# Layer 0's output projection in two PSUM banks in turn, more places for scores, and a new written order of the first fourteen positions

## What is computed

```python
out = concatenate([fourier_mix(f), ssd_out(y, z)], -1) @ w_out     # 1536 -> 1024
x = x + gate1 * out
h = rms_norm(x) * (1 + scale) + shift
# PEER, for each token and each of 8 heads
s = einsum("thsd,hskd->thsk", (h @ wq), keys)        # two sides, 128 scores each
s_top, i_top = top_k(s, 16)
g_score, c_idx = top_k(all 256 sums of one of each side, 16)
experts = e1 * 128 + e2;  gates = softmax(g_score)
act = gelu(u[experts] . h) * gates                   # 16 rows of u a head
y = sum(act * v[experts])                            # 16 rows of v a head
x = x + gate2 * y
```

## Time and profile before

| | us |
|---|---|
| median of 3 runs | 4380.73 (4378.84 to 4380.82) |
| the profiled execution | 4392.34 |
| its span | 4390.3 |
| layer 0's gathers are issued | 621.7 to 2678.8 |
| layer 1's gathers are issued | 3043.5 to 4357.3 |
| granted TensorE clock, mean | 0.843 |

### The profile page before, as it was taken

One profiled execution on the slowest core, in us unless ns is written; L12 is line 12 of the kernel. 1 busy time (PEld: TensorE's weight loads), 2 busy tenths in 40 slices (PEclk: granted clock), 3 DMA queues, 4 the chain that ended last, 5 costly groups with the idle time before them and its releaser, 6 DMA issues. The chain is left out here.

```text
span 4390.3 us, 37624 instructions
## 1 busy us (share of the span) xinstructions
PE 3099.0 (71%) x12112; PEld 1320.1 (30%) x12112; DVE 2858.1 (65%) x7086; ACT 1127.3 (26%) x2971; POOL 1579.2 (36%) x1383
## 2 busy tenths in 40 slices
PE   7999988776766765555566667999886755555555
PEld 3655543332322221111222213565432311111111
DVE  2524754789888988555555555565788898555554
ACT  1122521332322322111222212563332322111111
POOL 0002412344444455444444441001444454444443
PEclk9999998888887887777788878999987877777777
DMA  4114746799999999999999996103999999999998
GB/s 172 39 39 148 256 182 254 284 420 419 418 420 404 420 418 420 422 420 415 408 421 416 421 421 258 39 1 134 392 420 420 417 421 416 420 422 418 419 420 338
DMA packets 223656, 1471.78 MB, mean 335 GB/s; under 512 B 25436, under 2 KB 29244, under 8 KB 53220
## 3 DMA queue, kind: packets, MB, share of 16 engines
q0 software_dynamic: 184320, 1342.26, 74.0%
q1 hardware_dynamic: 37764, 123.17, 7.8%
q10 hardware_dynamic: 1376, 3.96, 0.2%
HBM read 1467.02 MB, written 2.28 MB: 335 GB/s over the span
## 5 line engine op out<-in xcount | busy, mean ns | idle before, releaser
L1911 PE MATMUL banks<-arena 128*64 128x512 f32 x5120 | 1640.6, 800 | 1188.0 <-ACT arena L2145 1132.0
L1643 POOL DMA_INDIRECT arena<-experts,arena x1280 | 1503.4, 1175 | 2293.8 <-PE banks L1911 1556.6
L2298 DVE CUSTOM_DVE_ANT_0 arena<-arena 128x1024 f32<-128x1024 f32 x1280 | 1535.0, 1222 | 834.1 <-DMA arena<-experts,arena 828.5
L1911 PEld LDWEIGHTS banks<-arena 128*64 128x64 f32 x5120 | 450.6, 182 | 2303.7 <-ACT arena L2145 1317.7
L2139 ACT ACTIVATE arena<-arena 128x4 f32<-128x4 f32 x320 | 66.1, 207 | 2296.1 <-DVE arena L2298 2279.8
L2145 ACT ACTIVATE arena<-arena 128x64 f32<-128x64 f32 x1280 | 340.4, 336 | 37.2 <-ACT arena L2139 1.2
L1734 PE MATMUL banks<-arena 128*128 128x512 f32 (+3 forms) x960 | 289.0, 456 | 6.2 <-DMA arena<-wq 5.2
L1661 PE MATMUL banks<-arena 128*128 128x512 f32 x416 | 197.2, 625 | 26.2 <-DVE arena L2191 22.4
L434 PE MATMUL banks<-arena 128*128 128x512 f32 (+1 forms) x640 | 210.1, 488 | 1.9 <-PEq L201 1.9
L871 POOL TENSOR_TENSOR arena<-arena 128x256 f32<-128x256 f32 x48 | 41.2, 859 | 433.3 <-POOLq L625 333.8
L1734 PEld LDWEIGHTS banks<-arena 128*128 128x128 f32 x960 | 160.7, 191 | 113.5 <-issue 87.9
(11 more groups left out here) (243 smaller groups left out, 2962.8 us busy)
## 6 DMA issues: line engine op xcount, KB each, us to landing
arena<-l_w_ada SPq DMA_DIRECT2D x48, 1024.0 KB, 5.0
arena<-wq SPq DMA_DIRECT2D x54, 512.0 KB
arena<-experts,arena POOLq DMA_INDIRECT x1280
arena<-l_w_in SPq DMA_DIRECT2D x7, 2048.0 KB, 7.8
arena<-l_w_out SPq DMA_DIRECT2D x4, 1536.0 KB, 8.8
arena<-l_w_o SPq DMA_DIRECT2D x4, 1024.0 KB, 9.9
arena<-keys SPq DMA_DIRECT2D x27, 128.0 KB
arena<-gates SPq DMA_DIRECT2D x6, 512.0 KB, 12.0
```

Source lines behind the costliest of these rows:

```text
L1643: pool.indirect_dma_start(slots[n], None, tbl, bass.IndirectOffsetOnAxis(ap=expert[:, ring[c], k:k + 1], axis=0)).then_inc(land[n]["sem"], ...
L1911: mm = pe.matmul(core["ps"][QS * j:QS * j + QS, c, :], diag[:, g % 2, k, :], v[:, D + c * 512:D + (c + 1) * 512], start=(g % (NB * PH) == ...
L2298: dve.tensor_tensor_reduce(u, u, rep[i // PH % 2][:, k % NQ, :], 1.0, 0.0, ALU.mult, ALU.add, dots[:, k:k + 1]).then_inc(dot["sem"], up(dot))
```

## The change

It leaves the computation and its amount as they are. In words:

- **Banks.** In layer 0, the first seven halves (up to (5,0)) go to banks 6 and 7 in turn: (0,0) 6, (0,1) 7, (1,0) 6, (2,0) 7, (3,0) 6, (4,0) 7, (5,0) 6. All the later ones, (1,1) to (5,1), are in bank 7 as before. `before_half` is now the last half before in the same bank.
- **Scores.** Events 2 to 7 of layer 0 have two tiles each and now use two of the four rows of a score buffer, by turns the upper and the lower ones; `scores_out` waits only for choices whose rows overlap. The query copy `qb` is split in two sides for events of two tiles too.
- **Order of the choices.** (4,0) comes fifth, before (2,1); seven choices instead of six, and six events instead of five, are done in the opening. The rule begins at position 14 with choice 7, so choice c is begun at position 2c where it was 2c - 1.
- **The written order** of all three engines is new. The projections stand some positions earlier on TensorE, `gate_out(5,1)` at the end of position 11 instead of 12, the dots are mingled with other work more finely, and softmaxes and diagonals on ScalarE stand in another order.

```diff
@@ PEER_MAPS, layer 0 @@
-     "order": [(0, 0), (1, 0), (2, 0), (3, 0)] + [c for h in range(4, PH) for c in ((h - 2, 1), (h, 0))] +
-              [(6, 1), (7, 1)] + [(7, t) for t in range(2, 6)] + [(0, t) for t in range(1, 6)] + [(1, 1)] +
-              [(h, t) for h in range(1, PH - 1) for t in range(2, 6)],
-     "choose_from": 11, "early": 6, "ahead": 5, ...
+     "order": [(0, 0), (1, 0), (2, 0), (3, 0), (4, 0)] + [c for h in range(5, PH) for c in ((h - 3, 1), (h, 0))] +
+              [(5, 1), (6, 1), (7, 1)] + [(7, t) for t in range(2, 6)] + [(0, t) for t in range(1, 6)] + [(1, 1)] +
+              [(h, t) for h in range(1, 5) for t in range(2, 6)] + [(5, 2), (6, 2)] +
+              [(h, t) for h in (5, 6) for t in range(3, 6)],
+     "choose_from": 14, "early": 7, "ahead": 6, "asked_from": 12, ... "halved": range(2, PH),
@@ peer_block @@
-        earlier[e] = max([n for n in range(e) if buffer_of[n] == buffer_of[e]], default=None)
+        first_tile = 2 * (e // 2 % 2) if e in m["halved"] else 0
+        rows_of[e] = range(first_tile, first_tile + len(events[e][1]))
+        before_e = [n for n in range(e) if buffer_of[n] == buffer_of[e] and set(rows_of[n]) & set(rows_of[e])]
+        earlier[e] = max([last[n] for n in before_e], default=None)
...
-    def bank_of(c):
-
+    def bank_of(t, c):
+
+        n = halves_at[t, c]
+        if layer == 0 and n <= halves_at[tiles - 1, 0]:
+            return 6 + n % 2
         return 6 + c
@@ TensorE, opening(g) @@
                 if g == 0:
+                    project(3, 0, 4, 10)
                     spread_choice(1)
-                    project(3, 0, 2, K)
-                    project(4, 0, 0, 4)
+                    project(3, 0, 10, K)
+                    project(4, 0, 0, 8)
                 if g == 1:
-                    project(4, 0, 4, K)
-                    project(5, 0, 0, 6)
+                    project(4, 0, 8, K)
+                    project(5, 0)
                 if g == 2:
-                    project(5, 0, 6, K)
                     project(1, 1)
+                    project(2, 1, 0, 4)
                 if g == 3:
-                    project(2, 1, 0, 4)
                     turn_rows(1)
-                    project(2, 1, 4, 8)
+                    project(2, 1, 4, 6)
+                    query(2, 0)
+                    project(2, 1, 6, 8)
                 if g == 4:
-                    query(2, 0)
                     query(2, 1)
-                if g == 5:
                     scores(2, 0)
                     scores(2, 1)
+                    project(2, 1, 8, 10)
                     query(3, 0)
+                    project(2, 1, 10, K)
+                    scores(3, 0)
...
@@ TensorE, the opening's rest, new @@
+                if g == 5: query(3, 1); project(3, 1, 0, 4); scores(3, 1); project(3, 1, 4, 6)
+                if g == 6: spread_choice(2); project(3, 1, 6, 10); query(4, 0); project(3, 1, 10, K)
+                if g == 7: query(4, 1); project(4, 1, 0, 4)
+                if g == 8: turn_rows(2); spread_choice(3); project(4, 1, 4, K); scores(4, 0); scores(4, 1)
+                if g == 9: project(5, 1, 0, 8)
+                if g == 10: project(5, 1, 8, K); query(5, 0)
+                if g == 11: turn_rows(3); scores(5, 0); query(5, 1); spread_choice(4)
+                if g == 12: turn_rows(4); scores(5, 1); turn_rows(5); spread_choice(5)
+                if g == 13: spread_choice(6)
@@ TensorE, ahead of position 0 @@
+                project(2, 0, 0, 2)
                 scores(1, 0)
-                project(2, 0, 0, 2)
                 scores(1, 1)
                 project(2, 0, 2, K)
-                project(3, 0, 0, 2)
+                project(3, 0, 0, 4)
@@ ScalarE, opening(g), new @@
+                if g == 0: softmax(1)
+                if g == 2: squares(1)
+                if g == 3: root(1); low_columns(1)
+                if g == 4: query_out(2, 0); query_out(2, 1); scores_out(2, 0); scores_out(2, 1); query_out(3, 0)
+                if g == 5: softmax(2); scores_out(3, 0); squares(2); query_out(3, 1)
+                if g == 6: scores_out(3, 1); root(2)
+                if g == 7: softmax(3); query_out(4, 0)
+                if g == 8: query_out(4, 1); squares(3); root(3)
+                if g == 9: scores_out(4, 0); scores_out(4, 1); squares(4); root(4)
+                if g == 10: softmax(4)
+                if g == 11: query_out(5, 0); low_columns(2); squares(5); root(5); softmax(5); query_out(5, 1)
+                if g == 12: low_columns(3); scores_out(5, 0); low_columns(4); scores_out(5, 1); softmax(6)
+                if g == 13: low_columns(5)
@@ VectorE, opening(g), new (d(a, b) stands for dot_batch(g, a, b)) @@
+                if g == 0: d(0, 4); choose_b(1); choice_out(1); gate_out(2, 0)
+                if g == 1: d(0, 1); gate_out(3, 0); d(1, 4)
+                if g == 2: d(0, 1); gate_identity(1); gate_identity(2); d(1, 2); gate_out(4, 0); d(2, 4)
+                if g == 3: d(0, 1); gate_out(5, 0); d(1, 3); gate_out(1, 1); d(3, 4)
+                if g == 4: d(0, 2); norm_rows(1); d(2, 3); high_columns(1); d(3, 4)
+                if g == 5: d(0, 1); gate_identity(3); d(1, 4); choose_a(2)
+                if g == 6: d(0, 1); gate_out(2, 1); d(1, 3); choose_b(2); d(3, 4); choose_a(3)
+                if g == 7: d(0, 1); choice_out(2); d(1, 4)
+                if g == 8: d(0, 1); norm_rows(2); gate_out(3, 1); gate_identity(4); d(1, 4); choose_b(3); gate_identity(5)
+                if g == 9: d(0, 3); norm_rows(3); high_columns(2); choice_out(3); d(3, 4)
+                if g == 10: d(0, 1); gate_out(4, 1); d(1, 2); choose_a(4); d(2, 4); norm_rows(4)
+                if g == 11: d(0, 2); choose_b(4); d(2, 4); gate_out(5, 1)
+                if g == 12: d(0, 1); choose_a(5); d(1, 3); high_columns(3); d(3, 4); gate_identity(6); choice_out(4)
+                if g == 13: d(0, 1); choose_b(5); norm_rows(5); d(1, 2); high_columns(4); choose_a(6); d(2, 3);
+                            gate_identity(7); d(3, 4); choose_b(6); choice_out(5); high_columns(5); choice_out(6)
```

More of the change, by code:

```diff
@@ L1312 @@
               [(h, t) for h in range(4) for t in range(1, 4)] + [(h, t) for t in range(2, 4) for h in range(4, PH)],
-     "choose_from": 3, "early": 2, "ahead": 4, "spread_at": (4, 5), "spread_first": (4, 5),
+     "choose_from": 3, "early": 2, "ahead": 4, "asked_from": 0, "spread_at": (4, 5), "spread_first": (4, 5),
      "halves": tuple((t, c) for t in range(TL) for c in range(2)),
-     "opening": tuple(range(8)) * 2, "ready": 8, "column": (), "near": 2,
+     "opening": tuple(range(8)) * 2, "ready": 8, "column": (), "near": 2, "halved": (),
      "w": RO + SLOT, "g1": HO + 16384, "g2": HO + 17408,
@@ L1370, in peer_block @@
     for e in range(AHEAD, E):
-        held = last[earlier[e]] if earlier[e] is not None else 0
-        query_at[e] = max(chosen_at[first[e], 0] - 5, query_at.get(e - 1, -1) + 2,
+        held = earlier[e] or 0
+        query_at[e] = max(chosen_at[first[e], 0] - 5, query_at.get(e - 1, -1) + 2, m["asked_from"],
                           chosen_at[held, 0] - 2 if held >= EARLY else 0)
@@ L1836, in opening @@
+                if g == 11:
+                    turn_rows(3)
+                    scores(5, 0)
+                    query(5, 1)
+                    spread_choice(4)
+                if g == 12:
+                    turn_rows(4)
+                    scores(5, 1)
+                    turn_rows(5)
                     spread_choice(5)
[L1837 to L1840 removed]
                 if g == 13:
[L1842 removed]
+                    spread_choice(6)
@@ L2058, in opening @@
             def opening(g):
+                if g == 0:
+                    softmax(1)
+                if g == 2:
+                    squares(1)
                 if g == 3:
-                    squares(1)
                     root(1)
@@ L2126, in _ @@
                 gate_low(3)
-                answer(1)
-                softmax(1)
+                query_out(1, 0)
+                query_out(1, 1)
+                scores_out(1, 0)
+                scores_out(1, 1)
             if layer == 1:
@@ L2404, in opening @@
+                    gate_out(3, 1)
+                    gate_identity(4)
+                    dot_batch(8, 1, 4)
                     choose_b(3)
-                    dot_batch(8, 1, 3)
-                    choice_out(3)
-                    gate_out(2, 1)
-                    dot_batch(8, 3, 4)
-                    choose_a(4)
+                    gate_identity(5)
                 if g == 9:
                     dot_batch(9, 0, 3)
-                    norm_rows(2)
-                    choose_b(4)
+                    norm_rows(3)
@@ L2436, in opening @@
-                if g == 13:
-                    dot_batch(13)
-                    norm_rows(5)
+                    choose_b(4)
+                    dot_batch(11, 2, 4)
+                    gate_out(5, 1)
+                if g == 12:
+                    dot_batch(12, 0, 1)
```

(23 more changed lines are left out.)

177 lines of the change are left out of this document (92 added, 85 removed).

## The result

The changed kernel took 4337.01 us in the median of four runs (4336.48 to 4340.26), the kernel before 4380.72 (4378.84 to 4380.82): ratio 0.9895, 95% interval 0.9883 to 0.9907. That is 43.7 us less, where 47 were forecast.

The account below looks back on a forecast made before the run. Transfers set the end, and layer 0's opening loop of slots and gathers withholds them. Gains of 16.7 + 18.3 + 16.7 less 2.1 make 49.6 us, taken as 47 off the 4380.7 median: 4334, range 4318 to 4345.

Parts of the forecast that it names:

- (a): The forecast itself: new banks and order in layer 0's opening give 4318 to 4345 us; chance 0.62.
- (b): Rival: alternated banks give nothing, since gathers end each turn anyway; the order's 32 us stay: 4349; chance 0.10.
- (d): Rival: no change, transfers not kept full after 806 us since VectorE enters position 13 late: 4381; chance 0.04.
- (e): Rival: slower, choices from position 14 wait longer for exponentials, 66 us lost against 50 gained: 4397; chance 0.04.
- (c): Rival: TensorE becomes the bound, a third of positions 4 to 9 at low clock: 24 gained, 4357; chance 0.18.
- the walk: Paper pass through each engine's written list with measured prices, over layer 0's opening: 49.6 us gained.
- to the worse side: Summed gain of 49.6 us, with 4 us better to 7 worse allowed, taken as 47.
- The clock of the forecast: Landing of the 53rd gather, first into the last five slots: the end moves with it, 49.6 us earlier.
- The banks: Positions 0 to 3: alternating banks hides the first halves, 3.7 + 13.0 = 16.7 us gained.
- Price nothing: Halved score buffers and longer `qb` only loosen waits; no VectorE or TensorE wait in the walk ends at them.
- Positions 5 to 7: TensorE's list sets these turns at 16.5, 13.3 and 13.0 us; position 5 gives back 5 us.
- The last gate: `gate_out(5,1)` closing position 11: the 53rd gather follows the 52nd by 1.3 us instead of 18.0, 16.7 gained.

Follow-up runs that it names:

- second profile: The changed kernel timed and profiled once more, nothing altered: 4340.5 us, ratio 0.9894 to the kernel before.
- four k moved: Changed kernel with four k of `project(4,1)` moved from behind block 8 to behind block 7: 4341.3 us, ratio 0.9893 to the kernel before.
- fewer k: Changed kernel with five of twelve k left out of each of halves (2,1) and (3,1): 4340.1 us, ratio 0.9888 to the kernel before.
- choice 2 early: Changed kernel with `spread_choice(2)`, `choice_out(2)` moved earlier and two k of `project(4,1)` moved behind block 7: 4343.2 us, ratio 0.9900 to the kernel before.

## Why the prediction was right, and where it was not

The time lay 3 us from the forecast, in case (a); (b), (d) and (e) did not occur. Of (c), TensorE's lists did set blocks 5, 6 and 7, as in the walk of (a), but the clock granted from 700 to 780 us was 0.96, where (c) asked for less than 0.85. A part of the closeness is luck: the walk gave 49.6, and the 2.6 us taken off it "to the worse side" had no row behind them.

**The clock of the forecast** was right, and is the best of it: the end moves with the 53rd gather. Ten kernels in eleven profiles show it. For the queue that stands before it 2.1 us were taken off; 45.9 us at the 53rd became 43.3 of length, 2.6 off (4.0 in the second profile).

**The walk.** Blocks after the first gather, forecast (with the 621.7 of before taken off) and measured: block 1 38.6 and 40.2, block 3 77.6 and 80.6, block 5 106 and 108.2, block 7 132 and 133.6, block 8 144 and 148.1, block 9 157 and 163.9, block 11 181 and 187.0, the 53rd 184.6 and 190.5. The sum of the walk, 49.6, was therefore 6 too large, and the 47 on record 3 or 4. Half of the 5.9 us at the 53rd had arisen by block 3. Position 1 took 1.1 us more than forecast, position 5 1.2 less; three turns hold most of the difference. Position 3, 1.5 us: the new wait for `gate_out(1,1)` was priced at 1.2, but the eight instructions behind it ran at the low level for a part. Position 8, 2.5 us: its landing took 9.5 us and not 6.9. Position 9, 2.8 us: block 8 had begun at the low level after 3.7 us of standing still. In the second profile these two turns are 1.2 to 1.3 us shorter. All are second-order costs of a wait, which the prediction had said that a walk does not see.

**The banks** were mis-sized: the prediction gave them the whole 16.7 us of positions 0 to 3. At block 3 the measured kernel is 13.7 us ahead, of which the banks' are 9.7 (taken from the new order) to 12.7 (put into the old one); the rest is the order's. The prediction also read all five of TensorE's waits, 22.4 us, as waits on bank 6. Three of them are, 20.1 us: the one of 5.75 at 641.43 and these two of the kernel before:

```profile
664.21 6.38 PE L1661 MATMUL banks<-arena 128*128 128x512 f32 x8 [6.17 <-DVE arena L2191]
...
689.36 7.47 PE L1661 MATMUL banks<-arena 128*128 128x512 f32 x12 [8.13 <-DVE arena L2191]
```

What the Trainium skill reports of a thin matmul kernel ("TensorE: Matmul & The Clock Gate", HAM oscillation in real kernels: double-buffering PSUM gave no further gain there) does not carry over: here 10 us were won, 10 of 4337, since the waits on the bank stood ahead of the blocks that free the slots.

**"Price nothing"** for the longer `qb` was wrong in this order: it is worth 7 to 9 us. The prediction looked for waits that the change removes from the old order; but a loosened wait has its price in the new one, where other work is put behind it. The halved score buffers were not tried alone, and the code says more of them than a price. With whole buffers `scores_out(4)` would wait for `choose_a(5)`, the last choice of event 2; on VectorE that stands behind `choose_a(4)`, which itself waits for `scores_out(4)`. The new order would never end. The buffers did not loosen a wait in it, they made it possible; this is read from the code, and no run shows it.

**Positions 5 to 7** took 15.8, 12.9 and 12.5 us, within 0.8 of TensorE's lists as priced (16.5, 13.3 and 13.0). The prediction called TensorE's list the bound, and it was, but with other bounds close behind it. The runs with four k moved and with fewer k took work from TensorE's path and gave most of what they won back within two positions; with choice 2 early a wait of GpSimd went, and 1.7 us of length were left. The changed kernel's transfers of 700 to 760 us (queue, packets, MB, share):

```profile
q0 software_dynamic: 2450, 17.88, 77.6%
q1 hardware_dynamic: 1146, 3.01, 13.1%
...
arena<-wq SPq DMA_DIRECT2D x6, 512.0 KB, 8.6
```

The query weights and keys of three events, 3.0 MB, share the engines with the gathers: 13.1% beside 77.6%. The walk had priced them at nothing. Over positions 4 to 8 they are 0.6 MB each, by my estimate 1.4 us at the 420 GB/s of the windows, beside four gathers' 10: 11.4 us of transfers a position, about the loop's 11.7 and close to TensorE's 12 to 13. Bounds of about the same length hide each other: easing one shows only the next. At position 7 the next is VectorE's list, as the rows in "Fewer k" show. At position 8, whose last dot waited for its landing, I take it to be the transfers; that is argued from their share, and no run took the weights away.

**The last gate**, the largest single step of the order, was priced at 16.7 us with its wait; moving it back by one position alone delays the 53rd by 9.5 to 12 us and costs 7.7 to 8.9 of length. The price held for the old order, where GpSimd waited 16.62 us for it; in the new one it waits 11.51.

No experiment gave a kernel that is measurably faster than the changed one.

## What to carry to other kernels

When a later stage runs at the full rate of one resource, find the event with which it begins; everything ahead of it is worth what it moves that event, here to within some 6 us over a range of 51. Walk the order by hand to the engine that issues the transfers, and add to each idle gap of TensorE the time that the instructions behind it lose at the low clock. Before moving a wait, read what would be late next, transfers of other queues included, and price an enabling edit (one that costs or saves nothing by itself, but lets other work be put elsewhere) inside the order that needs it, not in the old one.

## What was not expected of the hardware

Query weights of 512 KB landed 8.6 us (median, last row above) after their issue while gathers were queued, though such a transfer takes only 1.25 us of the engines, by an estimate at 420 GB/s. And gaps of TensorE as short as 2.3 us (before the projection at 692.59) were followed by instructions at the low level for a part, eight in 5.40 us instead of 3.6 (granted clock 0.68); the one of 1.03 us before block 2 was not.
